# Half jobs of an expert layer: gate and up in one chunk of 2048 columns by rows of 8 KB and one of 768, then all down pieces

## The reference, cut to what matters

```python
D_MODEL, SEQ, D_FF = 1024, 256, 2816
N_EXPERTS, TOP_K = 8, 2

def swiglu(t, w_gate, w_up, w_down):
    return (silu(t @ w_gate) * (t @ w_up)) @ w_down

def moe_ffn(u, router, w_gate, w_up, w_down):
    t = u.reshape(-1, D)
    top_v, top_e = lax.top_k(t @ router, TOP_K)
    top_w = softmax(top_v)
    # every token goes to its two experts; the results come back with its two weights
    out[token] += top_w[token, k] * swiglu(t[token], w_gate[e], w_up[e], w_down[e])
    return out

# h = h + moe_ffn(rms_norm(h, norm2_g)); the output is rms_norm(h, final_norm_g)
```

## Time and profile before

| | us |
|---|---|
| median of 3 runs (1117.83 to 1118.94) | 1117.89 |
| the profiled execution | 1117.7 |
| its span, first to last instruction | 1116.0 |
| TensorE busy | 1082.6 (97%) |
| VectorE busy | 701.4 (63%) |
| ScalarE busy | 634.6 (57%) |
| GpSimd busy | 306.5 (27%) |
| DMA engines, mean rate | 322 GB/s |

### The profile page before, as it was taken

The page is one execution under the profiler, slowest core; times in us unless marked ns, Lnnn a source line. Parts: engine busy times, 40 slices in busy tenths (PEclk is TensorE's granted clock), DMA queues, the critical chain, the costliest instruction groups (busy, mean ns, idle before and its releaser), DMA issues.

```text
span 1116.0 us, 14864 instructions
## 1 busy us (share of the span) xinstructions
PE 1082.6 (97%) x5739; PEld 829.6 (74%) x5739; DVE 701.4 (63%) x758; ACT 634.6 (57%) x756; POOL 306.5 (27%) x338
## 2 busy tenths in 40 slices
PE   7999999999999999999999999999988999999994
PEld 7888888888889877797348897897336898888331
DVE  4876555554568658996028889885016889888112
ACT  7878644443586876775027777774006777776002
POOL 9985200000087765583103003001003001200000
PEclk9999999999999999999999999999998999999998
DMA  9643985536234369999999999999999999999994
GB/s 303 200 158 97 403 316 187 189 111 200 82 110 151 133 243 410 400 411 405 402 414 405 405 414 407 405 413 409 406 412 406 409 411 409 407 408 409 414 403 199
DMA packets 114954, 359.28 MB, mean 322 GB/s; under 512 B 11509, under 2 KB 30127, under 8 KB 104640
## 3 DMA queue, kind: packets, MB, share of 16 engines
q1 hardware_dynamic: 108976, 344.16, 80.2%
q0 software_dynamic: 5728, 13.86, 3.6%
q10 hardware_dynamic: 176, 0.27, 0.1%
HBM read 352.17 MB, written 9.18 MB: 324 GB/s over the span
## 4 chain that ended last, share of the span: by engine, by line
PE 84%; DMA 7%; DVE 3%; ACT 3%; SPq 1%; issue 1%; DVEq 0%; ACTq 0%
PE bank L2843 9%; PE bank L2845 9%; PE bank L2844 9%; PE bank L2901 7%; PE bank L2870 5%; PE bank L2872 5%; PE bank L2871 5%; DMA ring<-in_moe_w_up_dram 4%; PE bank L2313 4%; PE bank L2314 4%; PE bank L2315 4%; DMA ring<-in_moe_w_down_dram 2%; PE bank L2430 2%; PE bank L2432 2%; PE bank L2333 2%; PE bank L2431 2%
## 5 line engine op out<-in xcount | busy, mean ns | idle before, releaser
L2185 DVE TENSOR_TENSOR ring_r<-ring,high 128x2048 fp32r<-128x2048 f32 x112 | 256.0, 2290 | 53.1 <-ACT high L1524 52.7
L1524 ACT ACTIVATE high<-ring 128x2048 fp32r<-128x2048 f32 x112 | 214.6, 1918 | 92.8 <-PE bank L2845 51.0
L2843 PE MATMUL bank<-high,uTh 128*128 128x512 f32 (+2 forms) x500 | 187.3, 375 | 5.8 <-DVE ring_r L2185 5.5
L2845 PE MATMUL bank<-high,uTl 128*128 128x512 f32 (+2 forms) x500 | 184.8, 370 | 0.0
L1089 ACT ACTIVATE high<-ring 128x2048 fp32r<-128x2048 f32 (+1 forms) x65 | 122.6, 1892 | 68.6 <-PE bank L2315 41.9
L875 POOL TENSOR_TENSOR low<-ring,high 128x512 fp32r<-128x512 f32 (+1 forms) x67 | 84.6, 1294 | 196.6 <-ACT high L1089 195.2
L1623 DVE TENSOR_TENSOR low<-ring,high 128x2048 fp32r<-128x2048 f32 (+2 forms) x38 | 85.6, 2257 | 54.8 <-ACT high L1089 52.2
L2844 PE MATMUL bank<-ring_r,uTh 128*128 128x512 f32 (+3 forms) x316 | 118.5, 375 | 0.0
L2843 PEld LDWEIGHTS bank<-high,uTh 128*128 128x128 f32 x500 | 94.6, 189 | 25.1 <-issue 7.0
L2845 PEld LDWEIGHTS bank<-high,uTl 128*128 128x128 f32 x500 | 94.5, 189 | 14.5
L1061 POOL DMA_INDIRECT expert_rows<-yrows,row_idx x5 | 6.8, 1358 | 343.6 <-ACT yrows L1480 343.6
(11 more groups left out here) (501 smaller groups left out, 2301.3 us busy)
## 6 DMA issues: line engine op xcount, KB each, us to landing
ring<-in_moe_w_down_dram SPq DMA_DIRECT2D x63, 1024.0 KB, 17.8
ring<-in_moe_w_up_dram SPq DMA_DIRECT2D x44, 1024.0 KB, 19.3
ring<-in_moe_w_gate_dram SPq DMA_DIRECT2D x44, 1024.0 KB, 19.0
ring<-in_w_in_dram SPq DMA_DIRECT2D x36, 512.0 KB, 5.3
low_raw<-in_moe_w_up_dram SPq DMA_DIRECT2D x12, 1024.0 KB, 19.1
low_raw<-in_moe_w_gate_dram SPq DMA_DIRECT2D x12, 1024.0 KB, 18.7
ring<-in_moe_w_up_dram SPq DMA_DIRECT2D x16, 768.0 KB, 19.2
ring<-in_ffn_w_up_dram SPq DMA_DIRECT2D x22, 512.0 KB, 5.4
```

The source lines that it names most:

```text
L1524: act.activation(high[:, p % SPLIT, :], moe_slot(j, p), ACT.Copy).then_inc(s["high_ready"], 1)
L2185: dve.tensor_tensor(moe_low(j, p), moe_slot(j, p), high[:, p % SPLIT, :].bitcast(F32), ALU.subtract).then_inc(s["low_ready"], 1)
L2843: pe.matmul(o, xh[:, k, :], bh, start=(k == 0), stop=False)
L2845: last = pe.matmul(o, xl[:, k, :], bh, start=False, stop=(k == KD - 1))
```

## The change

In half jobs (1, 4 and 7) the order of the pieces is up then gate of one chunk of 2048 columns, eight pieces each, up and gate of the ragged chunk, three each, then the eight down pieces of the first 2048 rows and the three of the rest. A piece of the first chunk is now one row block with rows of 8 KB. Inside, the 2048 columns are still worked as two parts of 1024, each with its own up and gate bank; with the ragged part's two banks, the result's bank and bank 7 of `own_slots`, all eight are in use. ScalarE's and VectorE's steps are put in the new order: both first parts one after the other, then, on VectorE in job 7, all four additions, then the ragged part. Transposes are placed after the last ragged up piece, after the last ragged gate piece and after the third down piece. The full jobs' order is as it was.

```diff
@@ -120,7 +120,20 @@
     return order + [("d", 1, i) for i in range(4)] + [("d", 2, i) for i in range(3)]
+def half_pieces():
+
+    u, g, d = ([(kind, 0, i) for i in range(8)] for kind in ("u", "g", "d"))
+    u2, g2, d2 = ([(kind, 2, i) for i in range(3)] for kind in ("u", "g", "d"))
+    return u + g + u2 + g2 + d + d2
+
+
+HALF_ORDER = half_pieces()
+HALF_AT = {key: p for p, key in enumerate(HALF_ORDER)}
+HALF_ENDS = (HALF_AT[("g", 0, 7)], HALF_AT[("g", 0, 7)], HALF_AT[("g", 2, 2)])
+HALF_TURNED = (HALF_AT[("u", 2, 2)], HALF_AT[("g", 2, 2)], HALF_AT[("d", 0, 2)])
+HALF_JOBS = (1, 4, 7)
 MOE_ORDER = moe_pieces()
+assert len(HALF_ORDER) == N_FFN
 MOE_AT = {key: p for p, key in enumerate(MOE_ORDER)}
 assert len(MOE_ORDER) == N_FFN
@@ -142,6 +155,10 @@
     return out
+def order_of(j):
+    return HALF_ORDER if isinstance(j, int) and j in HALF_JOBS else MOE_ORDER
+
+
 def landed(key):
     return 16 if key[1] < 2 or key in (("d", 2, 0), ("d", 2, 2)) else 32
@@ -168,7 +185,7 @@
     at = RING_PLACE[v]
     early = 32 * SLOT_OF[:-N_FFN].count(MOE_SLOTS[at]) if at < RING else 16 if at >= N_LOADED else 0
-    return early + sum(LANDED[g % N_FFN] for g in range(v, g_end, DEEP))
+    return early + sum(landed(order_of(g // N_FFN)[g % N_FFN]) for g in range(v, g_end, DEEP))
 def gates_end(c):
@@ -493,15 +510,14 @@
         DENSE_ACC = ((2, 3), (5, 6))
         MOE_UP, MOE_GATE, MOE_ACC = ((0, 1), (5, 6), (0, 1)), (4, 7), (2, 3)
-        HALF_UP, HALF_GATE, HALF_ACC = (0, 5, 0), 4, 2
+        HALF_UP, HALF_GATE, HALF_ACC = (0, 5, 1), (4, 6, 3), 2
+        HALF_SG = (0, 512, 0)
         OWN_BANK = 7
...
         WEIGHTS_AT = 16
-        HALF_JOBS = (1, 4, 7)
-
         JOB_AT = (0, 1, 4, 5, 2, 6, 7, 3)
         fin_g = unl_raw[:, 0:D]
@@ -515,7 +531,7 @@
         by_quad = xs.rearrange("p (b k) (q c) -> p q b k c", b=2, q=4)
         x_half = xT[:, :, 0:64]
-        hT_half = [half_hT[:, 4 * i:4 * i + 4, :] for i in range(2)]
+        hT_half = [half_hT[:, 0:4, :], half_hT[:, 4:8, :], xs[:, 0:3, :]]
         hT_full = [(moe_hTh, moe_hTl), (uTh[:, :, P:2 * P], uTl[:, :, P:2 * P])]
         pairs = spare[:, 0:4, P:2 * P].rearrange("p (t k) c -> p t k c", t=TT)
@@ -714,7 +730,8 @@
                 pick_e = lambda w: w[0, e:e + 1] if isinstance(e, int) else w[0, bass.ds(e, 1)]
                 wu, wg = (pick_e(w).rearrange("a (k p) n -> p (a k) n", p=P) for w in (moe_w_up, moe_w_gate))
                 wd = pick_e(moe_w_down).rearrange("a f n -> (a f) n")
-                for p, key in enumerate(MOE_ORDER):
+                whole = isinstance(j, int) and j in HALF_JOBS
+                for p, key in enumerate(order_of(j)):
                     kind, c, i = key
                     g = N_FFN * j + p
                     if not isinstance(j, int):
@@ -745,7 +762,9 @@
                                      [(dst, h1[:, D:3 * D])]][i]
                     else:
                         w, c0 = (wu if kind == "u" else wg), 1024 * c
-                        if c < 2:
+                        if whole and c == 0:
+                            parts = [(dst, w[:, i, 0:2 * 1024])]
+                        elif c < 2:
                             parts = [(both(0, 1024), w[:, 2 * i:2 * i + 2, c0:c0 + 1024])]
                         else:
                             parts = [[(both(0, 768), w[:, 0:2, c0:c0 + 768]), (dst[:, 1536:2048], w[:, 2, c0:c0 + 512])],
@@ -1571,20 +1590,30 @@
             def half(j, i, last=False):
                 result_rows(j, 2 * i)
-                for c in range(FULL_CHUNKS):
-                    w = HALF[c]
-                    act.wait_ge(s["piece_used"], used_of(j, gates_end(c)))
-                    act.activation(blocked(moe_sg[:, 0:w], c), strided(bank[HALF_GATE][:, 0:w], c),
+
+                def silu(c):
+                    w, at = HALF[c], HALF_SG[c]
+                    act.wait_ge(s["piece_used"], used_of(j, HALF_ENDS[c]))
+                    act.activation(blocked(moe_sg[:, at:at + w], c), strided(bank[HALF_GATE[c]][:, 0:w], c),
                                    ACT.Silu).then_inc(s["silu_ready"], 1)
-                    if c == 2 and not last:
-                        tokens_high(j + 1)
+
+                def hidden_out(c):
                     act.wait_ge(s["hid_tr"], 3 * j + (CHUNKS + c + 1))
-                    act.activation(hT_half[c % 2][:, 0:BLOCKS[c], :], bank[HALF_UP[c]][:, 0:w].rearrange("p (b n) -> p b n", n=P),
+                    act.activation(hT_half[c][:, 0:BLOCKS[c], :], bank[HALF_UP[c]][:, 0:HALF[c]].rearrange("p (b n) -> p b n", n=P),
                                    ACT.Copy).then_inc(s["hTh_ready"], 1)
-                    if c == 0 and not last:
-                        act.activation(wslot[:, :], twin_w[:, j:j + 1], ACT.Copy).then_inc(s["selT_ready"], 1)
-                    if c == 1 and last:
-                        own_slots(j, twin_w[:, j:j + 1])
+
+                silu(0)
+                silu(1)
+                hidden_out(0)
+                if not last:
+                    act.activation(wslot[:, :], twin_w[:, j:j + 1], ACT.Copy).then_inc(s["selT_ready"], 1)
+                hidden_out(1)
+                if last:
+                    own_slots(j, twin_w[:, j:j + 1])
+                silu(2)
+                if not last:
+                    tokens_high(j + 1)
+                hidden_out(2)
             for i in range(2):
                 act.wait_ge(s["first_T"], i + 1)
@@ -2216,13 +2245,13 @@
             def half(j, i, last=False):
                 for c in range(FULL_CHUNKS):
-                    w = HALF[c]
+                    w, at = HALF[c], HALF_SG[c]
                     dve.wait_ge(s["silu_ready"], 3 * j + 6 * i + (CHUNKS + 3 + c + 1))
-                    gated = blocked(moe_sg[:, 0:w], c)
+                    gated = blocked(moe_sg[:, at:at + w], c)
                     dve.tensor_tensor(gated, strided(bank[HALF_UP[c]][:, 0:w], c), gated, ALU.mult).then_inc(s["hid_ready"], 1)
-                    if last and c < 2:
-                        add_back(2 * c)
-                        add_back(2 * c + 1)
+                    if last and c == 1:
+                        for k in range(4):
+                            add_back(k)
                 if not last:
                     tokens_turned(j + 1)
                     tokens_low(2 * i + 1)
@@ -2894,44 +2923,57 @@
             def half(j, i, last=False):
                 def gates(name, c, q):
-                    p = MOE_AT[(name, c, q)]
+                    p = HALF_AT[(name, c, q)]
                     pe.wait_ge(moe_loaded[place_of(j, p)], landed_of(j, p))
-                    for k, h, a, b, at in segments(c, q):
-                        o = bank[HALF_UP[c] if name == "u" else HALF_GATE][64 * h:64 * h + 64, a:b]
-                        last = pe.matmul(o, x_half[:, k, :], moe_slot(j, p)[:, at:at + b - a], start=(k == 0), stop=(k == KD - 1))
+                    if (name, c, q) == ("g", 2, 0):
+                        pe.wait_ge(s["row_ready"], 2 * j)
+                    banks = HALF_UP if name == "u" else HALF_GATE
+                    if c == 0:
+                        for n in range(2):
+                            for h in range(2):
+                                at = 1024 * h + 512 * n
+                                last = pe.matmul(bank[banks[n]][64 * h:64 * h + 64, :], x_half[:, q, :], moe_slot(j, p)[:, at:at + 512],
+                                                 start=(q == 0), stop=(q == KD - 1))
+                    else:
+                        for k, h, a, b, at in segments(c, q):
+                            last = pe.matmul(bank[banks[c]][64 * h:64 * h + 64, a:b], x_half[:, k, :], moe_slot(j, p)[:, at:at + b - a],
+                                             start=(k == 0), stop=(k == KD - 1))
                     last.then_inc(s["piece_used"], 1)
...
                     for b in range(BLOCKS[c]):
-                        last = pe.transpose(bank[HALF_UP[c]][:, b * P:(b + 1) * P], moe_sg[:, b * P:(b + 1) * P], ident[:, :])
+                        last = pe.transpose(bank[HALF_UP[c]][:, b * P:(b + 1) * P], moe_sg[:, HALF_SG[c] + b * P:HALF_SG[c] + (b + 1) * P], ident[:, :])
                     last.then_inc(s["hid_tr"], 1)
                 def down(c, q):
-                    p = MOE_AT[("d", c, q)]
-                    if q == 0:
+                    p = HALF_AT[("d", c, q)]
+                    if c == 0 and q in (0, 2):
+                        pe.wait_ge(s["hTh_ready"], 3 * j + (CHUNKS + q // 2 + 1))
+                    if c == 2 and q == 0:
                         pe.wait_ge(s["hTh_ready"], 3 * j + (CHUNKS + c + 1))
                     pe.wait_ge(moe_loaded[place_of(j, p)], landed_of(j, p))
                     for part_of in range(2):
-                        h, b = divmod(2 * q + part_of, BLOCKS[c])
+                        if c == 0:
+                            h, at_hT, b = q // 4, q % 4 // 2, 2 * (q % 2) + part_of
+                        else:
```

(11 more changed lines are left out.)

## The result

| | before | after |
|---|---|---|
| median, us | 1117.89 | 1126.19 (6 runs, 1124.89 to 1127.32) |
| ratio, with its 95% interval | | 1.0074 (1.0064 to 1.0084) |
| profiled execution / its span, us | 1117.7 / 1116.0 | 1125.6 / 1123.8 |

A forecast was written before the change was run, and what follows sets the result against it. It took the end of the weight loads, plus a fixed tail, to bound the kernel. 1117.7 + 8.3 (additions) + 2.65 (clock) - 2.0 (rows) = 1126.65, with 0.2 to the median 1126.8 us; range 1120.7 to 1131.3.

The forecast's parts named there:

- (5): Job 7, VectorE: four additions, their loads one after another, delay the ragged product; TensorE stands 15 us, +8.3 us.
- (6): TensorE in job 7: its clock falls to half speed over the new wait, adding 2.65 us.
- (1): Half jobs' up and gate loads: rows of 8 KB move at 419 GB/s, gaining 1.0 us a job, 3.0 for three.
- rival C: Half jobs' loads: the longer rows bring nothing, jobs 5 and 6 start as before, 1128.8 us; chance 0.14.
- (2): Jobs 1 and 4: both load gains arrive at job 5's start, so jobs 5, 6 and job 7's start come 2.0 us earlier.
- A: Job 7: additions finish before the ragged product is wanted, with spacings of 4.6 us; 1114.9 us, chance 0.06.
- B: Job 7: the additions' loads are quick but not quick enough, spacings of 6.1 us; 1116.5 us, chance 0.04.
- D: TensorE in job 7: the wait is there but the clock stays up; 1124.1 us, chance 0.10.

The follow-up runs named there:

- early_adds_rows4: Changed kernel with job 7's additions moved as in early_adds, rows of 4 KB, products in turn on the two partition halves: 1118.02 us, 1.0001.
- early_adds: Changed kernel, but in job 7 addition 0 before product 0, addition 1 after product 1, additions 2 and 3 after the ragged product: 1115.16 us, 0.9976.
- two_tiles: Changed kernel, additions in their late place, but additions 1 and 3 take rows from a second tile, so two loads are out at once: 1115.35 us, 0.9977.
- three_adds: Changed kernel with additions 0, 1 and 2 ahead of the ragged product and addition 3 behind it: 1116.84 us, 0.9989.
- warm_wait: Changed kernel with 62 idle TensorE products in front of job 7's long wait: 1135.04 us, 1.0155.
- before_late_adds: Kernel before with all four additions after product 1, in front of the ragged product: 1122.57 us, 1.0042.
- after_rows4: Changed kernel, additions in their late place, with rows of 4 KB and products in turn on the two partition halves: 1127.98 us, 1.0089.
- warm_wait_33: Changed kernel with 33 idle TensorE products in front of job 7's long wait: 1123.81 us, 1.0055.

## Why the prediction was right, point by point

*The moved additions (5).* Shown: with them out of the way the loss is gone, with them alone in the old kernel there is one, with one less in front it shrinks by a spacing, and with a second tile it goes although they stay. By its steps, the first addition was put at 1066.8 - 2.0 = 1064.8 and came at 1064.72; the spacings at 28.6 in sum and came at 28.8 (9.73, 9.65, 9.44); the ragged product's end at 1095.2 and came at 1095.2; TensorE's wait at 15 us and came at 15.48. That the first addition met its time to 0.1 us is in part luck: job 7 began 1.83 us earlier and not 2.0, and the way from there to the addition took 30.0 us and not 30.3.

*The clock (6).* 2.65 was taken; it was 1.9 by the timelines and 2.4 by the medians. TensorE worked some 3.9 us at half speed, not 5.3.

*Rows of 8 KB (1).* The rate put for them, 419, came. Against the 407 that rows of 4 KB have in the same window of early_adds_rows4, a job's sixteen pieces (16.78 MB) take 40.0 us for 41.2, an estimate of 1.2 us in a job not disturbed, where 1.0 was put. The estimate from the Trainium skill's page "DMA: Bandwidth & Descriptors", section "Why small descriptors are slow", 0.5 us in a job, is less than half of that. The rule in that page's "Rules for kernel authors", that 128 partitions and 1 MiB are enough (rival C), is not borne out: the pieces were of that size on either side, and the rows still gave 2.9 us.

*What the gain moves (2): the step that was off.* Both gains were to arrive at job 5's start, 2.0 us. It came 1.26 us earlier, at 842.61 for 843.87. One pair of traces is a thin measure, but the others agree: the six with rows of 8 KB (this one, early_adds, two_tiles, three_adds and both of warm_wait) begin job 5 at 842.55 to 842.82, and the four with rows of 4 KB and fast products (before, before_late_adds, early_adds_rows4 and after_rows4) at 843.87 to 844.51, 1.5 us apart on average. For job 2 the traces tell nothing: 584.93 for 584.66, but 584.25 to 585.65 over the six. By the windows, part of job 1's gain was lost on the way. From 485 to 530 us its loads moved at 412 GB/s, for 407 before, where job 4's moved at 419. Windows from 520 to 530 us, before and after:

```profile
520.00:530.00 10.00, 10.00 (x47) 5.84 (x47) 2.79 (x2) 1.38 (x2) 2.14 (x3) 1.00 1.03 410
```

```profile
520.00:530.00 10.00, 10.00 (x47) 5.82 (x47) 2.77 (x2) 1.38 (x2) 2.17 (x3) 1.00 1.01 397
```

SyncE issued these loads one by one, 2.7 us apart, at the same times in both kernels, each as TensorE, still in job 0, gave a place free. A piece of 1.05 MB in 2.72 us is 385 GB/s, so here the stream can be faster only by what is already queued, and less was: the three single loads from 520 to 526 us landed 6.3 to 6.7 us after their issue, for 7.0 to 7.2 before. A stream that gets ahead there meets its 16 places full. That this is the cause was read and not tried.

The error was hidden in this execution: job 7 still began 1.83 us earlier (1034.70 for 1036.53), because the clock at job 5's start came back after 4.0 us of work and not 5.3, which is 0.6 us. That was luck. In the ten traces named above TensorE worked 3.0 to 5.5 us at half speed there, with the same products each time, and job 7's start comes 1.6 us earlier on average, not 2.0.

The sum was 1126.65 for the profiled execution's 1125.6. As the ragged product ended at the time that was put for it, all of this 1.05 lies behind it: 0.7 is the clock, 0.2 the transposes and eight pieces (14.6 put, 14.4 at full clock in warm_wait_33), and 0.1 to 0.2 the tail. The median lay 0.6 above the profiled execution, so the forecast of 1126.8 missed it by 0.6 only; as near as that is chance, since the changed kernel's runs spread over 2.4 us.

*The rivals.* A needed spacings of 4.6 us; they stayed over 9.4 beside rows of 8 KB as well, and B's 6.1 did not come either. C is answered under (1). What A promised without the chain, 1114.9, is what early_adds reached, 1115.16. D did not happen, the clock fell.

## What to carry to other kernels

When pieces are reordered, look for what shares an in-order engine with the step that is now needed earlier: a side task of a few us of work can hold that engine for its whole chain of loads, and a margin of 1 us in the old order says that the chain is already nearly in the way. Put such a task behind the urgent step, or give it a second buffer; either brought the gain that the change was to have. And a saving on a stream counts only where something waits for it: here part of job 1's did not arrive, it seems because the places were full, and with the late additions 1.1 of 2.9 us was lost under a later wait.

## What was not expected of the hardware

Products with 64 stationary columns gave one matmul record every 0.21 us when they went in turn to the two halves of the output partitions, and one every 0.43 us within a piece on one half (0.37 on average over 26 us), with the same 593 ns recorded for each. Over three jobs' sixteen pieces that was 46.6 us. A recorded duration does not show this, the count in a window does.
